# Experts placed from emptiest to fullest, with a new plan of the weight ring and the near rows gathered first, in a fused diffusion-trunk kernel

## The reference, cut to what matters

```python
def moe(h, w_router, router_bias, w_gate, w_up, w_down):
    s = jax.nn.sigmoid((h @ w_router).astype(jnp.float32))
    ...
    _, idx = lax.top_k(jnp.where(emask, sb, -jnp.inf), TOP_K)
    ...
    a = jnp.einsum('bsd,edf->bsef', h, w_gate)
    u = jnp.einsum('bsd,edf->bsef', h, w_up)
    act = jax.nn.silu(a) * u * gates[..., None].astype(h.dtype)
    return jnp.einsum('bsef,efd->bsd', act, w_down)
```

## Time and profile before

| | us |
|---|---|
| median of three timed runs | 1649.26 (1647.81 to 1649.79) |
| the profiled execution, its own time | 1657.81 |
| its span, first to last instruction | 1656.0 |
| TensorE busy | 1454.0 |
| VectorE, ScalarE, GpSimd busy | 556.2, 371.9, 226.7 |
| mean granted clock of TensorE, of full speed | 0.947 |

### The profile page before, as it was taken

One profiled execution on the slowest core, in us unless ns is written; L12 is line 12 of the kernel. 1 busy time (PEld: TensorE's weight loads), 2 busy tenths in 40 slices (PEclk: granted clock), 3 DMA queues, 4 the chain that ended last, 5 costly groups with the idle time before them and its releaser, 6 DMA issues.

```text
span 1656.0 us, 26585 instructions
## 1 busy us (share of the span) xinstructions
PE 1454.0 (88%) x10752; PEld 862.8 (52%) x10752; DVE 556.2 (34%) x1362; ACT 371.9 (22%) x985; POOL 226.7 (14%) x304
## 2 busy tenths in 40 slices
PE   3999998988997997997989999989869999969974
PEld 1876774323775774332564557743227766843221
DVE  1237343212456424211522442432105266242115
ACT  1106321110214521111211442211102045211110
POOL 0100122101121022111100001221011000221111
PEclk9999999998998998999899999999989999979997
DMA  9996148999788138899858403489997871247981
GB/s 328 320 320 196 77 173 292 384 413 349 262 304 233 78 134 280 305 421 349 296 197 246 120 1 153 173 298 387 399 345 258 280 270 55 98 164 302 422 338 56
DMA packets 122788, 417.21 MB, mean 252 GB/s; under 512 B 13659, under 2 KB 55614, under 8 KB 98086
## 3 DMA queue, kind: packets, MB, share of 16 engines
q1 hardware_dynamic: 95414, 345.08, 56.2%
q0 software_dynamic: 20304, 66.47, 12.2%
q10 hardware_dynamic: 6944, 3.91, 0.8%
HBM read 389.21 MB, written 28.76 MB: 252 GB/s over the span
## 4 chain that ended last, share of the span: by engine, by line
PE 70%; DVE 9%; DMA 8%; issue 6%; ACT 3%; POOL 1%; ACTq 1%; SPq 0%; another core or an unknown queue 0%; DVEq 0%; POOLq 0%
PE bank L1825 61%; DMA ring<-in_moe_w_gate 4%; PE bank L1995 3%; DMA hT<-h_rows,id_of 2%; PE bank L2159 2%; ACT pp L1147 2%; DMA ring<-in_moe_w_down 2%; ACTq L670 1%; PE bank L1882 1%; POOL small L804 1%; DVE xn L1294 1%; PE bank L2043 1%; DVE gbc L1291 1%; DVE xn L1304 1%; DVE hT L1281 0%
## 5 line engine op out<-in xcount | busy, mean ns | idle before, releaser
L1825 PE MATMUL bank<-ring,pp 128*32 128x512 f32 x2272 | 365.5, 634 | 40.6 <-DMA ring<-in_moe_w_down 27.9
L1825 PE MATMUL bank<-ring,hT 128*128 128x256 f32 (+3 forms) x998 | 234.9, 394 | 4.3 <-DVE kT L1590 2.6
L1825 PEld LDWEIGHTS bank<-ring,hT 128*128 128x128 f32 x998 | 182.5, 192 | 53.4 <-issue 27.9
L1825 PE MATMUL bank<-work,pp 128*32 128x512 f32 x816 | 183.9, 612 | 12.1 <-issue 9.2
L1825 PEld LDWEIGHTS bank<-ring,pp 128*32 128x32 f32 x2272 | 95.4, 116 | 167.1 <-issue 165.6
L1825 PE MATMUL bank<-ring,xn 128*128 128x256 f32 x768 | 168.2, 380 | 0.0
L1825 PEld LDWEIGHTS bank<-ring,xn 128*128 128x128 f32 x768 | 145.0, 190 | 19.4
L1825 PE MATMUL bank<-V,pp 128*32 128x512 f32 x512 | 131.0, 637 | 14.5 <-issue 11.6
L1715 DVE TENSOR_TENSOR pp<-bank,pp 128x256 f32<-128x256 f32 x40 | 17.0, 425 | 345.2 <-ACT pp L1224 345.2
L1147 ACT ACTIVATE pp<-bank,neg_max 128x384 f32<-128x384 f32 x192 | 96.6, 524 | 13.0 <-DVE neg_max L1606 10.1
L1825 PEld LDWEIGHTS bank<-work,pp 128*32 128x32 f32 x816 | 48.5, 112 | 94.5 <-issue 93.9
(11 more groups left out here) (275 smaller groups left out, 1800.1 us busy)
## 6 DMA issues: line engine op xcount, KB each, us to landing
ring<-in_w_mod SPq DMA_DIRECT2D x76, 1024.0 KB, 7.3
ring<-in_moe_w_gate SPq DMA_DIRECT2D x40, 1024.0 KB, 16.4
ring<-in_moe_w_up SPq DMA_DIRECT2D x40, 1024.0 KB
ring<-in_moe_w_down SPq DMA_DIRECT2D x37, 1024.0 KB, 14.5
work<-in_moe_w_down SPq DMA_DIRECT2D x16, 1024.0 KB, 7.9
y_slots<-kT POOLq DMA_DIRECT2D x32, 512.0 KB, 9.1
gbc<-in_w_mod SPq DMA_DIRECT2D x14, 1024.0 KB, 9.7
work<-in_moe_w_gate SPq DMA_DIRECT2D x12, 1024.0 KB
```

The lines of the kernel that those rows point to most:

```text
L1825: return pe.matmul(out, lhsT, rhs, start=start, stop=stop)
```

## The change

It places the eight emptiest experts right behind the fixed ones (places 4 to 11, 64 slots each, blocks 3 to 6) and the four fullest last (places 12 to 15, 96 each, blocks 7 to 9). The planner gets other times for the blocks. The route phase's modulation units are kept out of slots 0 and 1 and may take slot 13; down units of the last four places may take ten more slots. GpSimd issues the gathers of blocks 1 and 2 behind two of the six scatters, and SP's held weights wait for that (`near_issued`). VectorE makes `near` ahead of `held`, and copies the near ids ahead of its half of block 0's rows. TensorE runs `slot_ids` in the middle of `gather_rows`. The rest of the diff is the arithmetic in `places` that goes with it, a semaphore, and the wait for slot 13, which is the same in the route phase.

```diff
-SIZES = [WIDE] * (2 * FIXED) + [NARROW] * (E - 2 * FIXED)
+SMALL = E - 2 * FIXED
+SIZES = [WIDE] * FIXED + [NARROW] * SMALL + [WIDE] * FIXED
...
@@ unit_times @@
-        now += 73.0
+        now += 75.0
         for e in range(E):
             for part in ("moe_g", "moe_u"):
-                begin[part, L, e], end[part, L, e] = now + 11.8 * first_block(e), now + 11.8 * last_block(e) + 7.5
-            begin["moe_d", L, e] = now + 11.8 * first_block(e) + 11.0
-            end["moe_d", L, e] = now + 11.8 * last_block(e) + 18.5
-        now += 11.8 * BLOCKS + 20.0
+                begin[part, L, e], end[part, L, e] = now + 12.05 * first_block(e), now + 12.05 * last_block(e) + 7.4
+            begin["moe_d", L, e] = now + 12.05 * first_block(e) + 18.3
+            end["moe_d", L, e] = now + 12.05 * last_block(e) + 22.8
+        now += 12.05 * BLOCKS + 19.0
...
@@ homes @@
     if name == "moe_d":
-        return [(slot,) for slot in (6, 7, 12) + ((13,) if last_block(key[2]) < 7 else ())]
-    if name == "wo" or phase == "route" and key[2] == 1:
+        late = (13,) if last_block(key[2]) < 7 else tuple(range(6)) + (8, 9, 10, 11) if key[2] >= E - FIXED else ()
+        return [(slot,) for slot in (6, 7, 12) + late]
+    if name == "wo":
         return [(slot,) for slot in (4, 5, 6, 7)]
-    if name == "ukv" or phase == "route":
+    if phase == "route":
+        return [(2,), (3,)] if key[2:] in ((0, 0), (0, 1)) else [(slot,) for slot in (4, 5, 6, 7, 13)]
+    if name == "ukv":
         return [(slot,) for slot in (0, 1, 2, 3)]
...
@@ fill_expert (SP) @@
                     sp.wait_ge(held_ready, L + 1)
+                    sp.wait_ge(near_issued, L + 1)
...
@@ GpSimd @@
-                for b in range(NB):
+                def ids_by_slot(b):
                     for k in range(2):
                         nc.gpsimd.indirect_dma_start(ids, rows_at(row_of[:, k, b:b + 1]), own_id[:, b:b + 1], None,
...
+                ids_by_slot(0)
                 pool.wait_ge(h_out, 48 * (L + 1))
                 pool.wait_ge(ids_ready, L + 1)
...
                 block_in(1)
                 block_in(2)
+                pool.sem_inc(near_issued, 1)
+                ids_by_slot(1)
+                ids_by_slot(2)
                 later_ids()
...
@@ places (VectorE; the start and size of each place follow in the same number of instructions) @@
-                                      place_key[:, :].unsqueeze(2).to_broadcast([P, m, m]), ALU.is_gt))
+                                      place_key[:, :].unsqueeze(2).to_broadcast([P, m, m]), ALU.is_lt))
...
@@ VectorE's order @@
                 slot_rows(L, picks)
+                near_rows(L)
                 hold(L)
-                near_rows(L)
                 pick_weights(L, picks)
...
+                near_ids(L)
                 turned_rows(BLOCKS * L, 0)
-                near_ids(L)
...
@@ TensorE: gather_rows, and behind it @@
                     for k in range(KC):
+                        if k == KC // 2:
+                            slot_ids()
                         for b in range(NB):
...
                 gather_rows(BLOCKS * L)
-                slot_ids()
```

More of the change, by code:

```diff
@@ L239, in home_opens @@
         return mark[late[slot], L] if slot in late else 0.0
+    if part == "route":
+        return mark["mixed_in", L] if slot == 13 else 0.0
     return mark["summed", L - 1] if part == "main" and slot in (9, 13, 14) and L > 0 else 0.0
@@ L491, in build @@
              "ids_zeroed", "ids_out", "held_ready"))
-        near_ready, ids_full, ids_ready, ids_in, ov_t_in = (sem(s) for s in
-            ("near_ready", "ids_full", "ids_ready", "ids_in", "ov_t_in"))
+        near_ready, near_issued, ids_full, ids_ready, ids_in, ov_t_in = (sem(s) for s in
+            ("near_ready", "near_issued", "ids_full", "ids_ready", "ids_in", "ov_t_in"))
         g_in, y_out = [sem("g_in0"), sem("g_in1")], [sem("y_out0"), sem("y_out1")]
@@ L708, in home_free @@
                         sp.wait_ge(x_moe_v, 3 * L)
+                elif slot == 13 and part != "main":
+                    sp.wait_ge(wo_mul, 12 * (L + 1))
                 elif part == "moe":
-                    if slot == 13:
-                        sp.wait_ge(wo_mul, 12 * (L + 1))
-                    elif slot in (10, 11) and KINDS[L] < 2:
+                    if slot in (10, 11) and KINDS[L] < 2:
                         wait_evacuated(sp, *[("qT", L, p) for p in range(8)], *[("kT", L, g) for g in range(G)])
@@ L1418, in places @@
                                              in1=start_of[:, FIXED:E], op0=ALU.mult, op1=ALU.add))
-                link(V_.tensor_scalar(start_of[:, FIXED:E], start_of[:, FIXED:E], float(FIXED * WIDE), None, ALU.add))
+                link(V_.tensor_scalar(start_of[:, FIXED:E], start_of[:, FIXED:E],
+                                      float(FIXED * WIDE - SMALL * (WIDE - NARROW)), None, ALU.add))
                 link(V_.tensor_tensor(move_of[:, :], start_of[:, :], cap_of[:, :], ALU.add))
```

6 lines of the change are left out of this document (3 added, 3 removed).

## The result

The change makes the kernel faster, by less than half of what I forecast. The changed kernel takes 1634.24 us (median of 4 runs, 1628.52 to 1635.67), the kernel before, run beside it on the same chip, 1649.53 us (1647.81 to 1656.46): a ratio of 0.9893, 95% interval 0.9856 to 0.993, so 15 us gained between the medians, 18 by the ratio, where I expected 46. The profiled execution took 1635.19 us, with a span of 1633.4: 22.6 us less than the span before. Some 7 us of these are no gain of the change, since the profiled execution of before stood 8 us above its median and this one only 1.

What follows compares the result with a forecast made beforehand. The prediction took the expert stage to be bound by DMA's weight stream: 45.2 us there plus 1.4 in front (16.0 - 9.0 - 5.6) gave 46.6 saved and, scaled to the median, 1603 us, range 1577 to 1638.

Steps and rivals of the forecast that it cites:

- What bounds the stage: Expert stage, late blocks: TensorE waits for DMA; the weight stream at 417 GB/s stays the bound after the change.
- The 26 units: Weight stream: expert 15's up weights are the 26th 1 MiB unit behind expert 7's gate weights, taking 80.5 us.
- Rival (E): The stall only changes place: blocks 3 to 6 lose what blocks 7 to 9 lost, 22 us; 1649 us, chance 0.08.
- rival (B): Row gathers late behind an unbroken stream, at the transposes of blocks 4 to 9: 58 us, 1660 us, chance 0.06.
- rival (C): The weight stream runs slower, at 363 GB/s: 1641 us, chance 0.05.
- A to G, 45.2 us: From transposes behind block 2's gate-up (A) to VectorE's first combine (G): 45.2 us saved over four layers.
- the order of experts and the slots: Expert stage: blocks 7 to 9 need four held experts between them instead of two each; credited with 45.2 us.
- the last modulation unit: Front of three layers: next layer's eighth unit lands behind expert 3's weights, 3 us late each; -9.0 us, between 0 and 5.8 each.
- Rows of blocks 1 and 2, +16.0: Front: earlier gathers end block 1's row waits and cold gate-up; 16.0 us saved, between 0 and 17.6.
- The later list of ids: Moved scatters end 9 us later, delaying the id list for blocks 3 on; costed at 0.
- slot_ids, -5.6: Twelve small matmuls moved into the row gather delay it; -5.6 us in four layers, between 0 and -6.
- rival (A): The front gives nothing back, rows as late as now and modulation unit late: front -14.6, 1619 us, chance 0.12.

Runs made afterwards that it cites:

- Half the bytes: Changed kernel with the twelve held experts' weight units loaded by half, instructions and waits kept: 1588.71 us, one run.
- the repeats: The changed kernel and the kernel before, each run and profiled once more without edits: 1630.8 and 1650.8 us.
- the direct test: Changed kernel with old sizes, eighth modulation unit in ring slot 2, and experts 12 and 13's down weights ahead of expert 15's gate and up: 1615.23 us, ratio 0.9779.
- times and slots: Kernel before with two planner edits alone, measured block times and further slots for the last four experts' down weights: 1599.76 us, ratio 0.9685.
- the best version: Changed kernel with the old expert sizes and the eighth modulation unit in ring slot 2: 1588.21 us, ratio 0.9619.
- the change without the row part: Changed kernel with id lists, near-row gathers, slot lists and SP's wait as before; new sizes, planner and slots kept: 1635.66 us, ratio 0.989.
- the row part alone: Kernel before with only the GpSimd, VectorE and TensorE row edits and SP's wait; old sizes, planner and slots: 1657.54 us, ratio 1.0016.
- the unit in slot 2: Changed kernel with the eighth early modulation unit in ring slot 2, expert 3's gate and up following into slots 2 and 3: 1619.69 us, ratio 0.9776.

## Why the prediction was wrong, step by step

**What bounds the stage: right.** Half the bytes shorten A to G to 96.5 us on average, near the 94 that I had for a stage without waits, and the whole stream held 411 GB/s over 106 us. The 26 units, 80.5 us from g7's landing, put u15 at A + 85.6; it landed at A + 86.4, 85.3, 86.4 and 86.0. Rival (E) did not come: from A on TensorE stands for weights only from block 6. Nor did rival (B): the only wait for rows behind block 1 is the 2.3 us for block 3's. On the rule that spoke against this part, the Trainium skill, "DMA: Bandwidth & Descriptors", section Specifications, with some 358 GB/s per core: the trace is 15% above it, so rival (C) fell too.

**A to G, 45.2 us: 39.7, right in mechanism and near in size** (35.6 between the repeats). Waits for gate and up came in blocks 6 and 7, and the y rows released G in layers 0 to 2. Layer 3 was 3 us longer than forecast: from u15 to G I had 17 us there, and it took 20.2 (1580.99 to 1601.16). I had block 9's gate-up start when u15 lands, but TensorE was still at block 7's down then:

```profile
1579.55 3.64 PE L1839 MATMUL bank<-ring,pp 128*32 128x512 f32 x32
```

The gate-up began at 1583.56, 2.6 us behind u15, and from there G is 17.6 us away.

**What wins it: not asked.** I credited "the order of experts and the slots" together, because blocks 7 to 9 need fewer experts in the new order. I counted units by block and took 26 as given, and did not count the stream for the old order under the new planner. That count was in my reach: 24. The order of sizes costs 24 us of the stage (28.9 by the direct test), planner times and slots win some 61 (times and slots: 465.0 to 404.3).

**The failed step: the last modulation unit, "3 us late", -9.0.** The mechanism was there and the term too small. Counted from H, g3 and the unit were issued when I said, and TensorE wanted the unit when I said; but it landed 18.1, 17.1 and 20.0 us behind H where I had 16.6. From g3's issue to that landing (246.70 to 260.14) the core moved 330 GB/s, 4.4 MB in 13.4 us; I had counted 3.5 MiB, 3.7 MB, in 11.3. Whose bytes came in between was not taken apart. Of the 20.2 us of waits 19.6 are these three, 6.5 a layer in the mean, beyond even my bound of 5.8. The low clock came on top, which I had not priced: 4.27 us for half of the row gather. Taking the wait away shortens H to b1 by 18 us in the trace, twice my 9.0, and the kernel by 13 to 15 us in the medians.

**Rows of blocks 1 and 2, +16.0: nothing here.** The row part is worth 14.7 us in the best version, and nothing in this change or by itself. The 13.7 us of waits for block 1's rows did end. But I added this term to that of the late unit as if the two were independent: behind the late unit only 10.1 us of them were left to win, and TensorE reaches block 1's transposes 36.3 us behind H in layer 0, where it was 35.3. And what I took off for the waits that take their place, 1.6 us, was too little: against the change without the row part they are 4.0 us for VectorE's copies, 3.7 more for the turned rows and block 0's product, and 2.3 for block 3's rows. The later list of ids, which I costed at 0 with "a wait of up to 4 us there only lets the stream run ahead", is only the last of these here; in the row part alone it is 15.8 us. Behind A 2.8 us came back. Nor did the cold gate-ups of block 1 end (3.9 us of my term): 8.77 us against 7.07 in layer 0 and as much in layer 2. They do not hang on the late unit, since with the unit in slot 2 the granted clock between the transposes of blocks 1 and 2 is still 0.84 and 0.83 in these two layers.

**slot_ids, -5.6: nothing.** In layer 3, where no unit and no late row disturbs, H to b1 is 30.0 before and 29.9 after. There the 12 small matmuls delayed block 0's gate-up before as well, and now TensorE waits 0.98 us for the copies instead. In layers 0 to 2 TensorE stood 1.5 us behind them for the copies before and stands 0.98 now: in the row part alone block 0's gate-up begins no later behind H than before.

**The rest of the span, 0: some 6 us lost**, above. And I took the terms from one profiled execution, 8 us above its median; its repeat shows 9 us less from H to G, so part of what I wanted to win back was the spread of one execution.

With 39.7 gained, 10.4 lost in front and 6.7 in the rest, the profile gives 22.6 and the medians 15. My forecast for a front that gives nothing back, rival (A), was 1619: it needed also the loss in the rest.

## What to carry to other kernels

Ask of each part of a change what it would be worth alone, and what beside the others: here two planner edits give 52 us, and the order that they came with takes some 25 of that back. In a stage bound by a stream of loads, look first when the stream starts to run without a gap (9 us a layer here), then count the loads ahead of the last one that blocks the compute engine, for every order that is on offer; two loads more are two transfers more, in each pass. When a wait is taken away, look for the one right behind it. A load that comes late can be given another place in the queue or another slot: here the one was worth as much as the other, within the noise. An early gain in front of a late load is no gain until that load is in time.

## What the hardware showed that I had not expected

Four small scatters more ahead of the near rows' gathers in GpSimd's own queue made block 1 1.5, 2.9 and 2.5 us later in layers 0 to 2, though the engine issued them in time that was idle; some 4 us of head start for the weights in SP's queue made these rows land 0.3 to 2.5 us later and no difference in the total that could be measured (1624.2 against 1625.1 us). In 5.70 us of TensorE's idle the granted clock fell to 0.50, the lower of its two levels, and 24 matmuls behind it took 4.27 us in place of 2.92. And a single kernel spreads: 11 runs of the kernel before on one chip lay between 1645.6 and 1661.6 us, so the time of a single execution is no measure for terms of 5 us. Sums over four layers of one stage are steadier, but not exact either: H to b1, b1 to A and A to G differ by 4.0, 1.1 and 3.8 us between two executions of the kernel before, and by 4.1, 0.8 and 0.3 of the changed one.
